# A fused pair of transformer blocks on one core: own buffers and GpSimd's queue for the first weight units

## What is computed

```python
mod = (silu(c) @ ada_w + ada_b)            # 2048 x 12288, one row
sh1, sc1, g1, sh2, sc2, g2 = split(mod, 6)
h = rms_norm(x, norm1_g) * (1 + sc1) + sh1
proj = h @ w_in + b_in                     # 2048 x 11264; its first 2048 columns are u
u = causal_depthwise_conv(u, conv_w, conv_b)
y_lru = rg_lru(u, ...) * gelu(lru_gate)    # gates per head of 128, then a scan over tokens
```

## Time and profile before

| | us |
|---|---|
| median of 3 runs | 2838.43 (2834.81 to 2842.18) |
| profiled execution | 2836.98 |
| its span | 2835.2 |
| TensorE busy | 2741.1 |
| VectorE busy | 1957.6 |
| ScalarE busy | 1382.3 |

### The profile page before, as it was taken

One profiled execution on the slowest core, in us unless ns is written; L12 is line 12 of the kernel. 1 busy time (PEld: TensorE's weight loads), 2 busy tenths in 40 slices (PEclk: granted clock), 3 DMA queues, 4 the chain that ended last, 5 costly groups with the idle time before them and its releaser, 6 DMA issues.

```text
span 2835.2 us, 36852 instructions
## 1 busy us (share of the span) xinstructions
PE 2741.1 (97%) x14484; PEld 2333.4 (82%) x14484; DVE 1957.6 (69%) x2729; ACT 1382.3 (49%) x2070; POOL 11.1 (0%) x24
## 2 busy tenths in 40 slices
PE   7699999999999899999999999999989999999997
PEld 4588888888888788888888888887778888888886
DVE  6567767888897776555555567768567757766765
ACT  3137666554544554444444455544454434444443
POOL 0000000000000000000000000000000000000000
PEclk9899999999999999999999999999999999999999
DMA  7884566789987677555565555543545565555553
GB/s 281 284 305 147 164 212 202 255 277 358 342 293 259 230 260 236 193 186 187 188 194 188 181 190 183 192 134 127 181 159 188 193 194 185 185 193 184 189 192 127
DMA packets 161142, 596.69 MB, mean 210 GB/s; under 512 B 18087, under 2 KB 18248, under 8 KB 159624
## 3 DMA queue, kind: packets, MB, share of 16 engines
q1 hardware_dynamic: 158792, 579.37, 61.3%
q0 software_dynamic: 2176, 14.94, 1.4%
HBM read 590.05 MB, written 4.19 MB: 210 GB/s over the span
## 4 chain that ended last, share of the span: by engine, by line
PE 86%; DVE 6%; ACT 3%; DMA 3%; issue 2%; SPq 0%; POOL 0%; DVEq 0%; ACTq 0%
PE PS L634 85%; DMA W<-in_ada 2%; DVE WL L1692 2%; DMA W<-in_w_in 1%; ACT WH L1130 1%; DVE ACC L1695 1%; DVE G L1695 1%; DVE G L1692 1%; PE PS L773 0%; DVE G L1698 0%; DVE TT L1692 0%; DVE G L1994 0%; ACT TT L1389 0%; DVE XB L1692 0%; DVE XA L1692 0%
## 5 line engine op out<-in xcount | busy, mean ns | idle before, releaser
L634 PE MATMUL PS<-XA,WH 128*128 128x512 f32 (+1 forms) x4528 | 1599.8, 398 | 7.9 <-DVE WL L1692 4.3
L1692 DVE TENSOR_TENSOR WL<-W,WH 128x1024 fp32r<-128x1024 f32 x889 | 1081.0, 1223 | 597.9 <-ACT WH L1130 596.9
L634 PE MATMUL PS<-XA,WL 128*128 128x256 f32 x4488 | 1257.6, 280 | 0.0
L1130 ACT ACTIVATE WH<-W 128x1024 fp32r<-128x1024 f32 x889 | 930.8, 1055 | 526.4 <-PE PS L634 490.5
L634 PEld LDWEIGHTS PS<-XA,WH 128*128 128x128 f32 x4528 | 848.2, 188 | 212.9 <-DVE WL L1692 5.9
L634 PEld LDWEIGHTS PS<-XA,WL 128*128 128x128 f32 x4488 | 847.6, 189 | 2.3 <-issue 1.2
L634 PE MATMUL PS<-WH,XB 128*128 128x512 f32 x1440 | 446.6, 390 | 0.0
L634 PEld LDWEIGHTS PS<-WH,XB 128*128 128x128 f32 x1440 | 270.5, 188 | 56.3
L634 PE MATMUL PS<-WL,XB 128*128 128x512 f32 x720 | 280.1, 389 | 0.0
L1695 DVE SCALAR_TENSOR_TENSOR ACC<-W,SM,ACC 128x1024 f32<-128x1024 f32 x176 | 225.3, 1280 | 50.1 <-DMA W<-in_ada 47.4
L1172 ACT ACTIVATE EV<-PS 128x256 f32<-128x256 f32 x248 | 94.6, 383 | 315.0 <-PE PS L634 311.6
(11 more groups left out here) (209 smaller groups left out, 1487.9 us busy)
## 6 DMA issues: line engine op xcount, KB each, us to landing
W<-in_w_in SPq DMA_DIRECT2D x224, 512.0 KB, 4.9
W<-in_ada SPq DMA_DIRECT2D x192, 512.0 KB, 5.8
W<-in_w_ffn_in SPq DMA_DIRECT2D x176, 512.0 KB, 4.3
W<-in_w_up SPq DMA_DIRECT2D x176, 512.0 KB, 4.5
W<-in_w_ffn_out SPq DMA_DIRECT2D x88, 512.0 KB, 4.4
W<-in_w_down SPq DMA_DIRECT2D x88, 512.0 KB, 4.7
W<-in_w_lru_out SPq DMA_DIRECT2D x32, 512.0 KB, 5.3
W<-in_w_attn_out SPq DMA_DIRECT2D x32, 512.0 KB, 5.7
```

The costliest lines, as they stand in the source:

```text
L634: return e.matmul(o, l, r, start=start, stop=stop, skip_group_check=True)
L1130: return e.activation(o, a, ACT.Copy)
L1692: return e.tensor_tensor(o, a, b, op)
```

## The change

Slab entries have the ring to themselves; all 16 of slab 0 are VectorE's. Units 0 to 14 go to eight buffers WU, which are the four slots of WH and the four of WL seen as float32. GpSimd issues them: unit u when entry 16 (u // 5 + 1) + 2 (u mod 5) has landed and, from u = 8 on, unit u - 8 has been used. TensorE takes them at steps FIRST_AT. START is 69. The filter steps, the transposes and the loads of w3, ident, window and dft are at other places; the 25 small VectorE operations stand behind the opening; the gates of the LRU come one step later. NU, WHOLE and the units behind the opening are as they were.

```diff
-ADA_PE = (2, 5, 8, 11)
-UNITS_AFTER = (6, 8, 10, 12, 15)
-WHOLE = 12 * NU // 8
+FOUR = NU // 2
+WHOLE = 3 * FOUR
...
+FIRST = halves([("w_in", i) for i in range(NU)])
 def ring_plan():
-    start = halves([("w_in", i) for i in range(NU)])
-    plan = []
-    for q in range(4):
-        for k in range(KT):
-            plan.append(("ada", q, k // 2, k % 2))
-            if q and k in UNITS_AFTER:
-                plan.append(start.pop(0))
-    plan += start
+    plan = halves([("ada", q, j) for q in range(4) for j in range(8)])
+    plan += FIRST[WHOLE:]
...
-START = 4 * KT + 2 * NU
+START = 4 * KT + FOUR
...
-GATED = [c + 3 for c in CONV]
+GATED = [c + 4 for c in CONV]
...
-    WH = sb("WH", [P, USLOTS, UNIT], F32R)
-    WL = sb("WL", [P, USLOTS, UNIT], F32R)
+    WH, WHf = overlay(("WH", [P, USLOTS, UNIT], F32R), ("WHf", [P, USLOTS, UNIT], F32))
+    WL, WLf = overlay(("WL", [P, USLOTS, UNIT], F32R), ("WLf", [P, USLOTS, UNIT], F32))
+    WU = [x[:, i, :] for x in (WHf, WLf) for i in range(USLOTS)]
...
-        e.dma_start(w3, d["filt_w3_2"]).then_inc(*loaded["w3"]("w3"))
+        e.dma_start(IDN[:, :], d["ident"]).then_inc(*loaded["id"]("id"))
         for n, kind in enumerate(PLAN):
             if n >= RING:
                 m = n - RING
-                if m not in UNIT_OF:
-                    w.wait_ge(*(ape if m in ON_PE else adv)[m])
-                elif UNIT_OF[m] < WHOLE:
-                    w.wait_ge(*mm["unit", UNIT_OF[m]])
-                else:
-                    w.wait_ge(*lo[UNIT_OF[m]])
+                w.wait_ge(*(lo[UNIT_OF[m]] if m in UNIT_OF else adv[m]))
...
-            if n == RING - 1:
+            if n == 12:
+                e.dma_start(w3, d["filt_w3_2"]).then_inc(*loaded["w3"]("w3"))
+            if n == 14:
                 e.dma_start(win, d["window"]).then_inc(*loaded["win"]("win"))
-                e.dma_start(IDN[:, :], d["ident"]).then_inc(*loaded["id"]("id"))
+            if n == 30:
                 e.dma_start(CS, d["dft"]).then_inc(*loaded["cs"]("cs"))
...
     def pool(e):
         w = Waits(e)
+        for u in range(WHOLE):
+            n = KT * (u // FOUR + 1) + 2 * (u % FOUR)
+            w.wait_ge(*landed[n % RING][n])
+            if u >= len(WU):
+                w.wait_ge(*mm["unit", u - len(WU)])
+            _, tile, half = FIRST[u]
+            e.dma_start(WU[u % len(WU)], d["w_in"][tile][:, half * 1024:(half + 1) * 1024]).then_inc(
+                *first[u % len(WU)](u))
...
-        misc, early = Ring(MB[2:], BANK), Ring(GB, BANK)
+        misc = Ring(MB[2:], BANK)
...
                 if u < WHOLE:
-                    w.wait_ge(*landed[ENTRY[u] % RING][ENTRY[u]])
+                    w.wait_ge(*first[u % len(WU)][u])
...
         for n in range(START + 1):
-            if n in ON_PE:
-                ada(n)
             if n in SLAB_ENDS:
                 ada_sum(SLAB_ENDS[n])
             if n in X_STEPS:
                 next(xt)
             if n in FILTER_STEPS:
                 next(flt)
+            if n in FIRST_AT:
+                first_tiles(FIRST_AT[n])
             if n - 1 in UNIT_OF:
-                if n - 1 == ENTRY[0]:
-                    w.wait_ge(*fv["b", 3])
                 first_tiles(UNIT_OF[n - 1])
...
-            if n == 4:
+            if n == 6:
                 invert("x")
...
-X_STEPS = (12, 13, 14, 15, 46, 47, 48, 49)
-FILTER_STEPS = (3, 4, 6, 7, 16, 17, 18, 20, 22, 24, 26, 28)
+X_STEPS = (10, 11, 12, 13, 33, 36, 39, 42)
+FILTER_STEPS = (17, 21, 25, 29, 35, 38, 41, 44, 50, 53, 56, 59)
+FIRST_AT = {KT * (u // FOUR + 1) + (4, 7, 10, 13, 16)[u % FOUR]: u for u in range(WHOLE)}
```

More of the change, by code:

```diff
@@ L297 @@
     if _k[0] != "ada":
-        UNIT_OF[_i] = len(UNIT_OF)
-assert len(UNIT_OF) == NUNITS
+        UNIT_OF[_i] = WHOLE + len(UNIT_OF)
+assert len(UNIT_OF) == NUNITS - WHOLE
 ADA_END = {k[1]: i for i, k in enumerate(PLAN) if k[0] == "ada"}
@@ L304 @@
     ADA_SUM.setdefault(max(UNIT_OF[i] for i in range(ADA_END[_s]) if i in UNIT_OF) + 1, []).append(_s)
-ADA_LAST = {k[1]: i for i, k in enumerate(PLAN) if k[0] == "ada" and not (k[1] == 0 and 2 * k[2] + k[3] in ADA_PE)}
 ADA_OLD = {2: 0, 3: 1, 6: 2, 7: 3, 8: 6, 9: 7, 4: 8, 5: 9, 10: 4, 11: 5}
 ADA_ROW = (4, 5, 10, 11)
-START = 4 * KT + 2 * NU
+START = 4 * KT + FOUR
 CONV = [1 + 5 * h // 2 for h in range(16)]
-GATED = [c + 3 for c in CONV]
+GATED = [c + 4 for c in CONV]
 LAST = [GATED[4 * q + 3] for q in range(4)]
@@ L491, in _program @@
     landed = [signal(f"ring{i}", 16) for i in range(RING)]
+    first = [signal(f"first{i}", 16) for i in range(len(WU))]
     loaded = {k: signal("load_" + k, 16) for k in ("pv", "z", "w3", "cs", "win", "id", "x", "lw", "mask", "row1", "row2",
@@ L496, in _program @@
     mm = signal("pe_gemm")
-    ape = signal("pe_ada")
     red = signal("pe_ada_sum")
@@ L575, in sync @@
                 m = n - RING
-                if m not in UNIT_OF:
-                    w.wait_ge(*(ape if m in ON_PE else adv)[m])
-                elif UNIT_OF[m] < WHOLE:
-                    w.wait_ge(*mm["unit", UNIT_OF[m]])
-                else:
-                    w.wait_ge(*lo[UNIT_OF[m]])
+                w.wait_ge(*(lo[UNIT_OF[m]] if m in UNIT_OF else adv[m]))
             src = (d["ada"][kind[1], kind[2]] if kind[0] == "ada" else d[kind[0]][kind[1]])
             e.dma_start(W[:, n % RING, :], src[:, kind[-1] * 1024:(kind[-1] + 1) * 1024]).then_inc(*landed[n % RING](n))
-            if n == RING - 1:
+            if n == 12:
+                e.dma_start(w3, d["filt_w3_2"]).then_inc(*loaded["w3"]("w3"))
+            if n == 14:
                 e.dma_start(win, d["window"]).then_inc(*loaded["win"]("win"))
-                e.dma_start(IDN[:, :], d["ident"]).then_inc(*loaded["id"]("id"))
+            if n == 30:
                 e.dma_start(CS, d["dft"]).then_inc(*loaded["cs"]("cs"))
-    ON_PE = {n for n, k in enumerate(PLAN) if k[:2] == ("ada", 0) and 2 * k[2] + k[3] in ADA_PE}
     def pool(e):
         w = Waits(e)
+        for u in range(WHOLE):
[6 more added lines that the diff above has]
+                *first[u % len(WU)](u))
         w.wait_ge(*landed[(START - 1) % RING][START - 1])
@@ L634, in mul @@
             return e.matmul(o, l, r, start=start, stop=stop, skip_group_check=True)
[L636 to L645, removed]
         def ada_sum(s):
@@ L651, in ada_sum @@
                     w.wait_ge(*old)
-                    w.wait_ge(*adv[ADA_LAST[s]])
+                    w.wait_ge(*adv[ADA_END[s]])
                     mul(b, ONE[:, :], ACC[:, s % 2, chunk(i)], True, True).then_inc(*red(*([s, (s, i)] if i else [(s, i)])))
@@ L665, in ada_sum @@
             for i in range(8):
-                m = mul(b[:, c + i:c + i + 1], ACC[:, s % 2, i * P:(i + 1) * P], ONE[:, 0:1], s >= 4, True)
+                m = mul(b[:, c + i:c + i + 1], ACC[:, s % 2, i * P:(i + 1) * P], ONE[:, 0:1], s >= 4 or (s, i) == (0, 0), True)
             m.then_inc(*red(s))
@@ L686, in columns @@
             if u < WHOLE:
-                return W[:, ENTRY[u] % RING, c:c + n], None, ends
+                return WU[u % len(WU)][:, c:c + n], None, ends
             return WH[:, u % USLOTS, c:c + n], WL[:, u % USLOTS, c:c + n], ends
@@ L777, in layer @@
         def layer(i, l, r):
-            b, old = early.take(("layer", i), fv, ("layer", i))
+            b, old = misc.take(("layer", i), fv, ("layer", i))
             w.wait_ge(*old)
@@ L790, in filters @@
                 w.wait_ge(*loaded["w3"]["w3"])
-                b, old = early.take(("pf", n), fv, ("a", n))
+                b, old = misc.take(("pf", n), fv, ("a", n))
                 w.wait_ge(*old)
                 mul(b, l, w3[:, ch * 512:(ch + 1) * 512], True, True).then_inc(*flp(("f", n)))
-                b, old = early.take(("pb", n), fv, ("b", n))
+                b, old = misc.take(("pb", n), fv, ("b", n))
                 w.wait_ge(*old)
@@ L838, in tensor @@
         misc = Ring(MB, BANK)
-        misc.until = [(eu, ("u", NU - 1)), (md, 3), (cp, ("x", 7)), (sl, ("kf", 7))]
+        misc.until = [(eu, ("u", NU - 1)), (md, 3), (sl, ("kf", 7)), (sl, ("kf", 7))]
         def lru():
@@ L1267, in scalar @@
         for n in range(START):
-            if n in UNIT_OF and UNIT_OF[n] >= WHOLE:
+            if n in UNIT_OF:
                 high(UNIT_OF[n])
@@ L1703, in entry @@
                 s = u % USLOTS
-                if u < WHOLE:
-                    return
                 w.wait_ge(*hi[u])
@@ L1850, in vector @@
         filter_arg(0)
[L1851 to L1864, removed]
         filter_arg(1)
@@ L1952, in modulated @@
             return make
+        w.wait_ge(*sl["exp"])
+        chain(ts(lp[2], lp[1], 2.0, None, ALU.add))
+        chain(e.reciprocal(lp[2], lp[2]))
+        chain(tt(lp[2], lp[1], lp[2], ALU.mult))
+        chain(tt(lp[3], lp[2], lp[2], ALU.mult))
+        chain(ts(lp[4], lp[3], 1.0 / 19, 1.0 / 17, ALU.mult, ALU.add))
+        for k in (15, 13, 11, 9, 7, 5, 3, 1):
+            chain(tt(lp[4], lp[4], lp[3], ALU.mult))
```

(13 more changed lines are left out.)

## The result

| | before | after |
|---|---|---|
| median of runs, us | 2837.29 (2834.81 to 2842.18, 4 runs) | 2792.92 (2791.28 to 2800.22, 4 runs) |
| profiled execution, its span | 2836.98, 2835.2 | 2791.62, 2789.8 |
| T, start of TensorE's sum over partitions of slab 3 | 162.0 | 128.2 |
| first split matmul | 170.5 | 133.5 |
| span behind it | 2664.7 | 2656.3 |

The ratio is 0.9847, 95% interval 0.9824 to 0.9869: 37 to 50 us faster. The spans differ by 45.4 us: 33.8 of T, 3.2 between T and the first split matmul, 8.4 behind it.

The account below looks back on a forecast made before the run. TensorE was taken as the bound except in the opening, where its holds on the ring stop the loads. Savings of 34 + 2 + 5 = 41 us from 2836.98 gave 2796.0, or 2797.5 as the median; range 2784 to 2816.

Parts of the forecast that it names:

- SyncE waits for TensorE, and that is the hold: Opening: ring buffers held for TensorE stop SyncE's load stream; 88.4 us of SyncE waits, 18 times.
- T at 128: Opening: TensorE's sum over partitions of slab 3 starts at 128 us instead of 162, worth 34 us.
- T0: Opening: the end of slab 0's sums on VectorE, forecast at 35.2 us against 50.2 before.
- 390 GB/s: Opening: assumed rate of the load stream, between 406 in the best stretch and 358 sustained late.
- The GpSimd queue at nothing: Opening: issuing units from GpSimd makes TensorE wait 0 us, with an upper bound of 9.5 us per slab.
- Rival B: Opening: units come 9.5 us late by GpSimd's queue; T near 140, time 2809 us; chance 0.08.
- Rival C: Opening: VectorE's SBUF-to-SBUF work holds up each GpSimd issue; at 10 us each, T 192, time 2861; chance 0.04.
- 2 us between T and the split matmuls: Between T and the first split matmul: unit 15's high part copied before h saves 2 us, ends 0 and 4.
- Small operations ahead of unit 20 at nothing: Behind the opening: 25 small operations, 5.2 us, ahead of unit 20's low part cost nothing, up to 1 us.
- 5 us for the gates: LRU gates one step later: seven TensorE waits for a convolution's last tap, 7.0 us, go; worth 5, ends 0 and 7.
- Rival A: Opening: stream at 358 GB/s or TensorE units at 5.9 us; T 138 to 146, time 2807 to 2821; chance 0.16.
- Rival D: Behind the first split matmul: units 20 to 23 come late and return the gain; 2825 to 2838 us; chance 0.03.

Follow-up runs that it names:

- spread_only: Kernel before, with slab 0 all on VectorE, filters and transposes spread, gates one step later, units still in the ring: 2819.8 us, ratio 0.9942.
- w3late: Changed kernel with the loads of w3 and the window issued behind slab 0's entries: 2795.2 us.
- late_units: Changed kernel with GpSimd issuing each of units 0 to 14 four ring entries later: 2804.4 us.
- clumped: Changed kernel with filter steps, transposes of x and loads of w3, window and DFT matrix back near the front: 2808.1 us, ratio 0.9889.
- two crossed kernels: Changed kernel with the LRU gates at their old step, 2798.1 us; kernel before with only the gates one step later, 2833.5 us.
- repetition: Changed kernel, unaltered, timed again beside the last set of experiments: 2793.73 us.
- chain_first: Changed kernel with the 25 small VectorE operations put back between the two filter arguments: 2798.3 us.

## Why the prediction was right

2797.5 was forecast, 2792.9 measured, inside the range; the forecast case came about with its main mechanism, the hold on the ring. That T was met to 0.2 us is luck, since slab 0 was off by 5 us and slabs 2 and 3 made up for it. By its steps:

- **SyncE waits for TensorE, and that is the hold**: right. 88.4 us of such waits are gone, and spread_only, which keeps the units in the ring, keeps 65.7 of them and a T of 152.4.
- **T at 128**: 128.2. The parts under it were off and cancelled. T0 was forecast at 35.2 and came at 40.4: w3 and the window stand ahead of entries 13 to 15, and around w3 the stream runs at 176 GB/s; the step that took "16 x 1.33" for the stream of slab 0 left out these 1.6 MB. w3late, which moves them, ends slab 0's sums at 34.9, about the forecast number. Slab 1 was forecast at 31.9 us and took 31.8. Slabs 2 and 3 were forecast at 31.9 and 28.7 and took 29.5 and 26.4, since from its start to the start of the next a sum over partitions takes 1.7 to 1.8 us there, not 3.1, a unit 3.46 and not 3.6, a DFT step 1.7 and not 1.9, and a transpose 0.44 and not 0.8; only the first unit of slab 2 was longer, 5.2.
- **What bounds it**: the prediction had VectorE in slab 1 and TensorE in slabs 2 and 3, with the stream hidden by a little. The trace agrees for slab 1, where VectorE works from 48.65 us on without idle time, and for slab 2, whose sum TensorE reached last. It does not for slab 0, where VectorE waited 2.72 and 2.36 us for entries, nor for slab 3, where it waited some 6 us for entries and TensorE 0.36 us for it. So the stream is no longer hidden, and all three are within a few us of each other. The check by bytes, 46.1 MB at 390 GB/s, gave 121; it left out what is prefetched behind slab 3's last entry, 47.8 MB by 128 us in the windows above.
- **390 GB/s**: 384 to 396 from 35 us to T. The late stage's 358 did not bind. The Trainium skill gives about 358 GB/s as a core's limit, half of a memory stack's rate for each of two cores ("DMA: Bandwidth & Descriptors", section "Specifications"). It was no bound for this program on one core, which ran above it for 93 us on end.
- **The GpSimd queue at nothing**: right. An issue took 0.53 us, landings 7.1 and 7.8 us, the only wait for a unit 0.2 us. Rival B did not come about; late_units, whose units are late, bears out its price (T 138.0 and 2804.4 us, where B had T near 140 and 2809). Rival C did not come: beside SCALAR_TENSOR_TENSOR, which is most of VectorE's work here, an issue took 0.53 us. The lock that the Trainium skill describes ("SBUF — State Buffer", section "SBUF: two separate sides") may show once, in the issue of 0.85 us in clumped. One issue is no proof, and its 0.3 us cost nothing here.
- **2 us between T and the split matmuls**: 3.2, with unit 14 at 3.70 us instead of 5.88 and the sum before it at 1.95 instead of 3.10.
- **Small operations ahead of unit 20 at nothing**: right. The low part was ready at 146.9, 13.4 us behind the first split matmul. Their move is worth 3 to 4.6 us at the other end, which the prediction had inside T's 34 and not by itself.
- **5 us for the gates**: 3 to 4.5 by the two crossed kernels. Behind the first split matmul the profile has 8.4 us less, but its repetition 3.4 us: the rest is the difference between executions.

Rival A did not come about, though single units were as slow as it feared: 5.08 us at 47.98, and 5.39 at 74.11, where the granted clock was 0.69 in 74 to 79.5 us. Rival D did not either: WL waits are 2.3 us. The last of the signs of being wrong, a time behind the first split matmul that does not fall by about 5, lies within the scatter: it fell by 8.4 us in one execution and by 3.4 in the other.

## What to carry to other kernels

A ring's buffer is held by whoever reads it last: give data that must wait for something else a buffer outside the ring, and let the ring carry only what is used at once; which queue issues the loads came out the same. Then spread slow work of the consuming engine so that it never falls behind by more than the ring holds, and put nothing in front of its first use of the stream: where stream and engines are all near their limits to the end of a stage, as here, what was lost at its start stayed lost, and a change of order alone won nothing. And before costing a stage, look for loads that use few partitions.

## What was not expected of the hardware

w3 lies on 64 partitions. While it moved, the stream fell to 176 GB/s over 4 us with the DMA engines' share still at 0.95, against 406 in windows of tiles on 128 partitions (24 to 28 us of w3late, 20 to 25 of the earlier trace rows); with w3 issued later the dip came later. The window, which is loaded next to w3 there and lies on 128 partitions, can be told apart in the kernel before: w3 is issued at 3.2 us and lands 10.7 us later, and 10 to 12 us runs at 184 GB/s; the window lands near 24 us, with 385 GB/s in 22 to 24 us. The Trainium skill has the rule, "SBUF — State Buffer", section "Door 1: The DMA port swizzle (why `[64,N]` ≈ `[32,N]`)": partitions 0 to 63 reach only 8 of 16 ports. The trace agrees, with somewhat under half the full rate, though loads on 128 partitions stood around w3 in the queue.

Second, a sum over partitions of the same 16 instructions took 3.54 us behind 11 us of idle time and 1.84 to 1.95 behind at most 1.7 us of it. The idle time alone does not decide it: in the kernel before, the four sums took 3.54, 3.57, 1.95 and 3.10 us behind 1.80, 2.90, 1.79 and 1.65 us of it. Nor does the granted clock that the profile shows: it is 1.00 in 40.5 to 44 us of the changed kernel and 0.50 (1.2 of 2.4 GHz) in 43.5 to 47 us of chain_first, where the same sum took 3.55 us. The cause stays open.
